# Hybrid encoder layer on one core: the input projection's x tiles 2 to 11 turned in 32x32 blocks on VectorE instead of on TensorE, the per-token scale moved to the evictions, and alternating PSUM banks

## The chip, the core and the metric

The program runs on one of the eight cores of a Trainium2 chip. A core has a matrix engine (PE, TensorE; PEld is its weight load), two engines that read and write both SBUF and PSUM (DVE, VectorE; ACT, ScalarE), a third vector engine that works in SBUF (POOL, GpSimd), a queue engine (SP) that here only issues DMAs, and 16 DMA engines. They run on their own and meet through semaphores. The metric is the device time of one execution in microseconds (us). Three executions of the kernel before took 1500.43, 1500.71 and 1501.08 us; the median is 1500.71.

## The reference, cut to what matters

One encoder layer in fp32 over a prompt of 512 tokens and a sample of 1024 tokens (1536 tokens, 12 tiles of 128), model width 1024. The change touches the part down to `proj`:

```python
h = rmsnorm(x, norm1_g)              # x * rsqrt(mean(x*x) + eps) * g
proj = h @ w_in                      # 1024 -> 1280 columns
q, k, v = proj[..., :512], proj[..., 512:640], proj[..., 640:768]
u = proj[..., 768:]                  # 512 columns for the pooling mixer
q = apply_axial_rope(rmsnorm(q, q_norm_g), cos, sin)   # per head of 64
k = apply_axial_rope(rmsnorm(k, k_norm_g), cos, sin)
a = block_swept_gqa(q, k, v)         # softmax attention, 8 q heads, 2 kv heads
p = multiscale_pool(u, w_pool, pool_scale)
x = x + concatenate([a, p]) @ w_out
x = x + square(relu(rmsnorm(x, norm2_g) @ w_up)) @ w_down
```

The token's factor rsqrt(mean(x*x) + eps) is the same for all columns of a token, so it can multiply x before the product or q, k, v and u behind it. The gain g belongs to the rows of w_in.

## The kernel before

**How the precision is kept.** Every fp32 product is made of three products of operands rounded to a shorter format: an operand is split in a rounded half (hi) and the rest (lo), and PE does hi·hi, hi·lo and lo·hi (helper `three`, lines 794 to 796). For the weights ACT writes `wihi` (the rounding, with g as its scale) and DVE `wilo` (what is left); for the tokens ACT writes `hThi` and DVE `hTlo`.

**The projection, tile by tile.** PE contracts over partitions, so each tile of x (128 tokens on partitions) has to be turned to have the 1024 model columns on partitions, as 8 blocks of 128 columns. For tile t:

- ACT squares x and sums along the row (`square_x`, L1240), POOL makes the factor `rsx` of it (`norm_x`, L2298 and L2300);
- DVE writes `xs` = x times that factor (`scale_x`, L1742);
- PE turns `xs` with 8 transposes of 128x128 into PSUM banks 0 and 1 (`transpose_x`, L803; for tile 0 L878);
- ACT rounds the result from PSUM to `hThi`, DVE takes the difference to `hTlo` (`split_hT`, L1232 and L1736);
- `project_qkv`: 48 matmuls in PSUM banks 2 and 3 give the 768 columns of q, k and v, with tokens on partitions. For each 2 tiles `project_u` gives the 512 columns of u in banks 4 and 5, with the columns on partitions and 256 tokens along the row, in four groups g of 24 matmuls.

**Behind the product.** ACT copies q and k to `qk` (`copy_qkv`), which also gives banks 2 and 3 free: the next `project_qkv` waits for `qk_copied`. ACT squares, DVE sums the squares (`sum_squares`, L1826), POOL takes the power -1/2 (`rsqk`, L2300), DVE scales (`scale_qk`, L1832) and multiplies by the gain (`gain_qk`, L1837), and then the rotation: DVE writes `roped` with the cosines (L1845), POOL writes `qsin` (L2376), DVE adds it (L1849). Then PE turns `roped` with 5 transposes (`transpose_qk`, L919) into banks 6 and 7, and ACT saves them in `QT`. u is copied from PSUM to `up` by ACT (`save_u_columns`).

**The order of the work.** It is written out by hand, engine by engine; every engine takes its instructions in order. PE's order for a pair of tiles t (even) and t+1 is: `project_qkv(t)`, `transpose_x(t+2)`, `project_qkv(t+1)`, `transpose_x(t+3)`, `project_u` of the pair with `transpose_qk(t)` ahead of its third group, `transpose_qk(t+1)`. DVE's order for a tile is V, `sum_squares(t)`, `split_hT(t+2)`, `scale_x(t+3)`, `scale_qk(t)`, `gain_qk(t)`, `rotate(t)`. The start differs: PE warms up with matmuls on zeros (L1052, twice 7), turns the column of g and tile 0, and runs tile 0 in step with the splits of the weights (`first_qkv`, L828 to L837), then tile 1 (L865 to L870); and DVE has `split_wi_u`, the rest of the weights' split (L1766), to do for the first `project_u`. In the last tiles the first attention scores are mixed into `project_u`. Behind the projection come attention (with POOL normalizing the probabilities and computing the pooling windows), the output projection and the MLP, which runs from about 600 us to the end. The change leaves them as they are.

## Time and profile before

| | |
|---|---|
| median of 3 executions | 1500.71 us (1500.43 to 1501.08) |
| span of the profiled execution, first to last instruction | 1499.2 us |
| PE busy | 1490.5 us (99% of the span) |
| DVE, ACT, POOL busy | 1015.6 (68%), 718.0 (48%), 394.7 us (26%) |
| input projection | from the start to about 200 us |

The profiled execution is one of its own; the profile gives its span and no device time beside it, and the span is 1.5 us below the median of the timed ones. In the page, "busy" is the union of an engine's instructions, and "mean ns" of a group is what one instruction took with its latency, which for pipelined matmuls is more than the distance from one start to the next. "[0.33 <-DVE xs L1742]" behind an instruction says that its engine had been idle for 0.33 us and what released it. The granted clock of PE is given as a share of full speed for each stretch; which level a matmul ran at is also seen in its own rhythm.

### The profile page before, as it was taken

What the parts mean: (1) busy time and instruction counts of PE and PEld (TensorE: products, weight loads), DVE (VectorE), ACT (ScalarE), POOL (GpSimd) and SP (SyncE); (2) the same over time, 40 slices, a digit from 0 to 9 for tenths busy, and PEclk for the clock granted to TensorE, in tenths of its full rate; (3) what the DMA queues carried; (4) which work ended last, traced back from release to release, by engine and by line L of the source; (5) the groups of instructions that cost most, each with busy time, mean ns of one, the idle gap of its engine ahead of it and who ended that gap; (6) DMA issues with size and microseconds to landing.
All of it is one profiled execution on the core that took longest, in us unless ns stands there. A gap on an engine that the chain in (4) does not pass through costs nothing.

```text
span 1499.2 us, 23419 instructions
## 1 busy us (share of the span) xinstructions
PE 1490.5 (99%) x8031; PEld 1328.7 (89%) x8031; DVE 1015.6 (68%) x1287; ACT 718.0 (48%) x1215; POOL 394.7 (26%) x348
## 2 busy tenths in 40 slices
PE   9999999999999999999999999999999999999999
PEld 8999988888878889999999999999888888888887
DVE  7434489999965567445445444548888878878875
ACT  6323289999943335555445455546332323223220
POOL 3356379988940000000000000000411311311300
PEclk9999999999999999999999999999999999999999
DMA  6110021100145737523333432438743443442434
GB/s 237 50 36 18 18 78 29 29 11 11 33 171 182 266 142 305 236 101 143 135 128 112 156 138 101 146 132 314 266 151 119 133 154 104 143 158 94 144 99 182
DMA packets 69113, 195.19 MB, mean 130 GB/s; under 512 B 5560, under 2 KB 7744, under 8 KB 68928
## 3 DMA queue, kind: packets, MB, share of 16 engines
q1 hardware_dynamic: 66992, 183.36, 34.8%
q10 hardware_dynamic: 2064, 11.08, 1.8%
q8 instruction: 35, 0.57, 0.2%
q14 instruction: 22, 0.18, 0.0%
HBM read 119.97 MB, written 67.63 MB: 125 GB/s over the span
## 4 chain that ended last, share of the span: by engine, by line
PE 93%; ACT 2%; POOL 2%; DVE 1%; issue 1%; DMA 0%; SPq 0%; ACTq 0%; POOLq 0%; DVEq 0%
PE ps L794 24%; PE ps L796 23%; PE ps L795 23%; PE ps L1096 6%; PE ps L974 4%; PE ps L1106 3%; PE ps L956 2%; PE ps L958 2%; PE ps L989 2%; PE ps L990 2%; ACT prob L1327 1%; PE ps L1116 1%; PE ps L803 1%; POOL prob L2401 0%; ACT pThi L1232 0%
## 5 line engine op out<-in xcount | busy, mean ns | idle before, releaser
L794 PE MATMUL ps<-h,wuhi 128*128 128x384 f32 (+1 forms) x904 | 301.3, 333 | 0.2 <-issue 0.2
L796 PE MATMUL ps<-h,wulo 128*128 128x384 f32 (+1 forms) x904 | 301.1, 333 | 0.0
L795 PE MATMUL ps<-h,wuhi 128*128 128x384 f32 (+1 forms) x904 | 301.1, 333 | 0.0
L794 PE MATMUL ps<-wdhi,hidhi 128*128 128x512 f32 x672 | 261.5, 389 | 0.1
L796 PE MATMUL ps<-wdhi,hidlo 128*128 128x512 f32 x672 | 261.4, 389 | 0.0
L795 PE MATMUL ps<-wdlo,hidhi 128*128 128x512 f32 x672 | 261.4, 389 | 0.0
L2202 DVE TENSOR_TENSOR yacc<-yacc,ps 128x1024 f32<-128x1024 f32 x167 | 203.3, 1217 | 77.1 <-PE ps L796 77.0
L1232 ACT ACTIVATE hidhi<-hin 128x1024 fp32r<-128x1024 f32 (+1 forms) x72 | 86.9, 1207 | 300.8 <-PE ps L796 291.7
L2116 DVE TENSOR_TENSOR u<-u,ps 128x384 f32<-128x384 f32 x96 | 53.1, 553 | 181.2 <-PE ps L796 181.1
L794 PEld LDWEIGHTS ps<-h,wuhi 128*128 128x128 f32 x904 | 169.7, 188 | 0.6 <-issue 0.4
L795 PEld LDWEIGHTS ps<-h,wuhi 128*128 128x128 f32 x904 | 169.7, 188 | 0.0
L796 PEld LDWEIGHTS ps<-h,wulo 128*128 128x128 f32 x904 | 169.7, 188 | 0.0
L794 PEld LDWEIGHTS ps<-wdhi,hidhi 128*128 128x128 f32 x672 | 126.2, 188 | 26.9 <-issue 0.5
L796 PEld LDWEIGHTS ps<-wdhi,hidlo 128*128 128x128 f32 x672 | 126.2, 188 | 26.1
L795 PEld LDWEIGHTS ps<-wdlo,hidhi 128*128 128x128 f32 x672 | 126.2, 188 | 26.0
L2573 POOL TENSOR_TENSOR hout<-h,hout 128x384 f32<-128x384 f32 x1 | 1.8, 1774 | 477.2 <-PE ps L796 477.2
L1736 DVE TENSOR_TENSOR hidlo<-hin,hidhi 128x1024 fp32r<-128x1024 f32 (+1 forms) x72 | 113.0, 1569 | 5.4 <-ACT hidhi L1232 5.4
L1736 DVE TENSOR_TENSOR pTlo<-ps,pThi 128x512 fp32r<-128x512 f32 x160 | 107.3, 687 | 13.3 <-ACT pThi L1232 11.4
L1563 ACT ACTIVATE hout<-u 128x384 f32<-128x384 f32 x96 | 50.5, 526 | 124.9 <-DVE u L2116 113.5
L1232 ACT ACTIVATE pThi<-ps 128x512 fp32r<-128x512 f32 x160 | 95.0, 600 | 18.8 <-PE ps L974 13.4
L974 PEld LDWEIGHTS ps<-ident,prob 128*128 128x128 f32 x640 | 78.3, 140 | 25.7 <-DVE pTlo L1736 3.1
L2401 POOL TENSOR_SCALAR prob<-prob,rinv 128x1024 f32<-128x1024 f32 (+1 forms) x96 | 94.4, 995 | 22.5 <-DVE rinv L1815 20.7
(221 smaller groups left out, 2822.1 us busy)
## 6 DMA issues: line engine op xcount, KB each, us to landing
hd<-hout SPq DMA_DIRECT2D x64, 384.0 KB, 3.2
hin<-hd SPq DMA_DIRECT2D x48, 512.0 KB, 3.7
hd<-hout SPq DMA_DIRECT2D x32, 576.0 KB, 2.8
hin<-hd SPq DMA_DIRECT2D x24, 768.0 KB, 4.3
wuraw<-in_w_up SPq DMA_DIRECT2D x17, 1024.0 KB, 6.0
wdraw<-in_w_down SPq DMA_DIRECT2D x8, 2048.0 KB, 9.5
h<-h2d ACTq DMA_DIRECT2D x7, 1536.0 KB, 10.9
x2in<-in_x SPq DMA_DIRECT2D x12, 512.0 KB, 3.4
```

The costliest lines, as they stand in the source:

```text
L794: pe.matmul(out, w_hi, m_hi, start=start, stop=False, skip_group_check=resumed)
L795: pe.matmul(out, w_hi, m_lo, start=False, stop=False, skip_group_check=resumed)
L796: return pe.matmul(out, w_lo, m_hi, start=False, stop=stop, skip_group_check=resumed)
L974: mm = pe.transpose(ps[:, 4 + k % 3, qt * P:(qt + 1) * P], prob[s.parity(pair, idx)][:, u, c0:c0 + P], ident[:])
L1096: pe.matmul(ps[:, 2 * i + h], c[i][:, k], wohi[:, j, h * 512:(h + 1) * 512], start=(j == 0 and c is chi), stop=False)
L1106: mm = pe.matmul(ps[:, 2 * i + h], chi[i][:, SLOT_ROWS[j]], wolo[:, j, h * 512:(h + 1) * 512], start=False, stop=(n == KT - 1))
L1232: return act.activation(out, in_, ACT.Copy, **kw)
L1563: act.activation(out, src, ACT.Relu).then_inc(relu_done, 1)
L1736: return dve.tensor_tensor(out, a, b.bitcast(F32), ALU.subtract)
L2116: dve.tensor_tensor(u, u, up_bank(par, (1, 4, 5)[k]), ALU.add).then_inc(u_sum, 1)
L2202: dve.tensor_tensor(q, q, down_banks(u, o), ALU.add).then_inc(acc_done, 1)
L2401: ins = pool.tensor_scalar(p, p, rinv[:, b, q:q + 1], 1.0, ALU.mult, ALU.mult)
```

## The change

- The model columns are dealt to partitions in another way: partition p now holds columns 8p to 8p+7, the eighth k of them in block k (before: block k holds columns 128k to 128k+127). w_in and g are loaded to fit.
- Tiles 2 to 11: SP loads x in four quarters of 256 columns to 32 partitions each (`load_x`), so that DVE can make the whole turn of 128x1024 by one STREAM_TRANSPOSE of 32x32 blocks, from SBUF to SBUF (`turn_x`). Its input is read at steps of 8 elements. `scale_x` and `transpose_x` go. `split_hT` reads `xT` in SBUF.
- Tiles 0 and 1 are turned on PE as before, but unscaled and from columns 8 elements apart (`row_in`), and without waiting for the squares.
- The squares of tiles 2 to 11 need rows of x that a second DMA brings (`load_rows`).
- The token's factor `rs` is now kept for all tiles and multiplies q, k and v when ACT and DVE take them from PSUM. For u it has to lie along the row: two DMAs for each pair of tiles write two columns of `rs` to DRAM and read them back to all partitions (`turn_rs`, `rsb`), and DVE, not ACT, takes u from PSUM, multiplied by it.
- `project_qkv` alternates between banks 0, 1 and 2, 3.
- At the start: 8 warming matmuls, not 14, and no transpose for g.

The core of the diff:

```diff
--- before.py
+++ after.py
+        rs = at("rs", X + 2048, [TT])
+        g1c = at("g1c", 1408, [KT])
+        rsb = at("rsb", X, [2, 2 * P])
+        rsd = nc.dram_tensor("rsd", [TT // 2, P, 2], F32).ap()
...
+        xT = at("xT", W + 8192, [KT, P])
...
-            k0, k1, bank = ((0, 2, 5), (2, 4, 0), (4, 8, 1))[h]
+            k0, k1, bank = ((0, 2, 6), (2, 4, 7), (4, 8, 2))[h]
...
+        def turned(t):
+            return psw[:, 2048:3072].rearrange("p (k c) -> p k c", k=KT) if t == 1 else xT[:]
+        def row_in(i, k):
+            return xin[:, i].rearrange("p (c k) -> p k c", k=KT)[:, k]
+        def quarter_in(i, q):
+            return xin[q * 32:q * 32 + 32, i].rearrange("t (b c) -> t b c", b=4)
+        def quarter_of(t, q):
+            return x[t * P:(t + 1) * P, q * 256:q * 256 + 256].rearrange("(b t) c -> t b c", b=4)
+        def blocks_in(i, k0=0, k1=KT):
+            return xin[:, i].rearrange("p (b c k) -> p k b c", b=4, k=KT)[:, k0:k1]
+        def blocks_out(k0=0, k1=KT):
+            return xT[:, k0:k1].rearrange("p k (b t) -> p k b t", b=4)
...
+        def stat_area():
+            return up[:, :, UPW - PAD - 256:UPW - PAD]
+        def qkv_banks(i):
+            return 2 * (i % 2)
+        w_rows = w_in.rearrange("(p k) n -> k p n", k=KT)
...
-                sp.wait_ge(xs_done, t - 1)
-                sp.dma_start(xin[:, i], x[bass.ds(t * P, P)]).then_inc(x_in[i], 16)
+            def load_x(t):
+                sp.wait_ge(xT_done, t - 1)
+                if t < 4:
+                    sp.wait_ge(ssx_done, t - 1)
+                for q in range(4):
+                    sp.dma_start(quarter_in(t % 2, q), quarter_of(t, q)).then_inc(x_in[t % 2], 16)
+            def load_rows(t):
+                sp.wait_ge(ssx_done, t)
+                sp.dma_start(stat_area(), x[t * P:(t + 1) * P].rearrange("t (g c) -> t g c", g=GROUPS)).then_inc(xn_in, 16)
...
+            def turn_rs(p):
+                sp.wait_ge(rsx_done, 2 * p + 2)
+                sp.dma_start(rsd[p], rs[:, 2 * p:2 * p + 2]).then_inc(rs_out, 16)
+                if p >= 2:
+                    sp.wait_ge(u_saved, FIRST + p - 1)
+                sp.wait_ge(rs_out, 16 * (p + 1))
+                if p:
+                    sp.wait_ge(rs_in, 16 * p)
+                sp.dma_start(rsb[:, p % 2], rsd[p].rearrange("t i -> (t i)").partition_broadcast(P)
+                             ).then_inc(rs_in, 16)
...
+            sp.dma_start(xin[:, 0], x[0:P]).then_inc(x_in[0], 16)
...
-            sp.wait_ge(x_in[1], 16)
...
-            load_x(2, 0)
...
+            load_wi_u(0)
+            load_wi_u(1)
             sp.dma_start(gqkb[:], gqk.partition_broadcast(P)).then_inc(gqk_in, 16)
-            sp.dma_start(rope[:, 0], rope_d[0]).then_inc(rope_in[0], 16)
-            sp.dma_start(rope[:, 1], rope_d[1]).then_inc(rope_in[1], 16)
-            load_x(3, 1)
+            load_rope(0)
+            load_x(2)
+            load_rope(1)
+            load_rows(2)
+            load_x(3)
+            turn_rs(0)
...
+            for t in range(TT):
+                if t + 4 < TT:
+                    load_x(t + 4)
+                if t + 3 < TT:
+                    load_rows(t + 3)
+                if t % 2 and t + 2 < TT:
+                    turn_rs((t + 1) // 2)
+                if t + 2 < TT:
+                    load_rope(t + 2)
...
-            def transpose_x(t):
-                pe.wait_ge(xs_done, t + 1)
-                pe.wait_ge(hT_lo, t)
-                for k in range(KT):
-                    mm = pe.transpose(psw[:, k * P:(k + 1) * P], xs[:, k * P:(k + 1) * P], ident[:])
-                mm.then_inc(xT_done, 1)
...
+            def project_qkv(t, i):
+                buf, tok, bank = i // 2, (i % 2) * P, qkv_banks(i)
+                pe.wait_ge(hT_lo, t + 1)
+                pe.wait_ge(qk_copied, FIRST + t - 1)
...
+                for k in range(KT):
+                    if k == 5:
+                        pe.wait_ge(x_in[1], 16)
+                        for c in range(KT):
+                            mm = pe.transpose(turned(1)[:, c], row_in(1, c), ident[:])
+                        mm.then_inc(xT_done, 1)
+                    if k in (0, 2):
+                        pe.wait_ge(hT_hi_half, 1 + k // 2)
                     if k == 4:
                         pe.wait_ge(hT_hi, 1)
+                    high(k)
+                    if k in (0, 2):
+                        pe.wait_ge(hT_lo_half, 1 + k // 2)
+                    if k == 4:
                         pe.wait_ge(hT_lo, 1)
-                    high(k)
                     cross(k)
-                    if k == 5:
-                        transpose_x(1)
-                    mm = low(k)
-                mm.then_inc(qkv_done, 1)
+                    if k:
+                        low(k - 1)
+                low(KT - 1).then_inc(qkv_done, 1)
...
-                transpose_x(2)
-                def between(g):
-                    if g == 2:
-                        pe.wait_ge(v_lo, FIRST + 2)
-                        transpose_x(3)
-                    if g == 3:
-                        transpose_qk(0, 0)
-                pe.wait_ge(qk_copied, FIRST + 2)
-                project_u(0, 0, between)
+                project_u(0, 0, lambda g: transpose_qk(0, 0) if g == 3 else None)
...
-                transpose_x(4)
                 project_qkv(3, 3)
-                transpose_x(5)
...
-                    project_qkv(t, i, 0 if last and i == 2 else 2)
-                    if not (last and i >= 2):
-                        transpose_x(t + 2)
+                    project_qkv(t, i)
...
-            warm(7)
...
+            split_first(0)
+            act.wait_ge(g1_in, 16)
             split_wi(0)
-            split_first(0)
+            split_first(1)
             split_wi(1)
-            split_first(1)
+            split_first(2)
             split_wi(2)
-            split_first(2)
             split_wi(3)
             split_wi(4)
-            square_x(1, 1)
-            for k in range(5, KT):
-                split_wi(k)
+            square_x(0)
+            split_wi(5)
             split_hT(1, 1)
-            square_x(2, 0)
+            split_wi(6)
+            split_wi(7)
+            square_x(1)
...
+                copy(qk[:].rearrange("p h d -> p (h d)"), psw[:, bank * 512:bank * 512 + QKW],
+                     scale=rs[:, t:t + 1]).then_inc(qk_copied, 1)
+                copy(V[:, t, :, 0:HEAD], ps[:, bank + 1, P:2 * P].rearrange("p (v d) -> p v d", v=NKV),
+                     scale=rs[:, t:t + 1]).then_inc(v_hi, 1)
...
-            def save_u_columns(n, i):
-                p = n * 2 + i // 2
-                act.wait_ge(u_done, FIRST + p + 1)
-                act.wait_ge(pads, 1)
-                if isinstance(n, int) and p == TT // 2 - 1:
-                    act.wait_ge(ssx_done, TT)
-                copy(up[:, :, bass.ds(p * 256 + PAD + 2 * PAD * ((n + 1) // 2), 256)],
-                     psw[:, 2048:3072].rearrange("p (g c) -> p g c", g=GROUPS)).then_inc(u_saved, 1)
...
-            def scale_x(t, i):
-                dve.wait_ge(rsx_done, t + 1)
-                dve.wait_ge(xT_done, t)
-                dve.tensor_scalar(xs[:], xin[:, i], rsx[:, 0:1], 1.0, ALU.mult, ALU.mult).then_inc(xs_done, 1)
+            def turn_x(t):
+                dve.wait_ge(x_in[t % 2], 64 * (t // 2) + 16)
+                dve.wait_ge(hT_hi, t)
+                dve.wait_ge(hT_lo, t)
+                dve.transpose(blocks_out(), blocks_in(t % 2)).then_inc(xT_done, 1)
...
+            def save_u_columns(p):
+                dve.wait_ge(u_done, FIRST + p + 1)
+                dve.wait_ge(rs_in, 16 * p + 16)
+                dve.wait_ge(pads, 1)
+                if p == TT // 2 - 1:
+                    dve.wait_ge(ssx_done, TT)
+                c0 = p * 256 + PAD + 2 * PAD * (p >= SEQ_P // 256)
+                dve.tensor_tensor(up[:, :, c0:c0 + 256].rearrange("p g (i t) -> p g i t", i=2),
+                                  psw[:, 2048:3072].rearrange("p (g i t) -> p g i t", g=GROUPS, i=2),
+                                  rsb[:, p % 2].rearrange("p (t i) -> p i t", i=2).unsqueeze(1).to_broadcast([P, GROUPS, 2, P]),
+                                  ALU.mult).then_inc(u_saved, 1)
...
-                scale_x(2, 0)
                 for k in range(KT // 2):
                     split_wi_u(k)
                 scale_qk(0)
                 for k in range(KT // 2, KT):
                     split_wi_u(k)
-                split_v(1, 5)
                 dve.wait_ge(gq_scaled, 1)
                 gain_qk(0)
+                split_v(1, 3)
                 sum_squares(1)
+                rotate(0, 0)
+                turn_x(2)
                 split_hT(2, 2)
-                scale_x(3, 1)
-                rotate(0, 0)
                 scale_qk(1)
                 gain_qk(1)
+                turn_x(3)
+                rotate(1, 1)
                 split_hT(3, 3)
-                rotate(1, 1)
-                scale_x(4, 0)
+                turn_x(4)
+                save_u_columns(0)
...
-                        scale_x(t + 3, (i + 3) % 2)
+                    if t + 3 < TT:
+                        turn_x(t + 3)
...
+                    if i % 2 and not (last and i == 3):
+                        save_u_columns(t // 2)
...
+            save_u_columns(TT // 2 - 1)
...
-                    if not (last and i >= 1) and not opens:
-                        norm_x(t + 3)
...
+                    if t + 2 < TT:
+                        norm_x(t + 2)
```

DVE, the first pair of tiles behind the split of the weights, before (`qn<-qk,rsqk` is scale_qk(1), the last two rows are rotate(1) but for its neighbours; the number behind a name is its buffer):

```order
L1736 TENSOR_TENSOR V<-ps,V 128x2x64
L1837 TENSOR_TENSOR qn<-qn,gqkb 128x640
L1826 TENSOR_REDUCE ssqk<-qksq 128x10
L1736 TENSOR_TENSOR hTlo_83<-ps,hThi_81 128x8x128
L1742 TENSOR_SCALAR xs<-xin,rsx 128x1024
L1845 TENSOR_TENSOR roped<-qn,rope 128x640
L1849 TENSOR_TENSOR roped<-roped,qsin 128x640
L1832 TENSOR_TENSOR qn<-qk,rsqk 128x640
L1837 TENSOR_TENSOR qn<-qn,gqkb 128x640
L1736 TENSOR_TENSOR hTlo_83<-ps,hThi_81 128x8x128
L1845 TENSOR_TENSOR roped<-qn,rope 128x640
L1849 TENSOR_TENSOR roped<-roped,qsin 128x640
```

The same place now:

```order
L1842 TENSOR_TENSOR qn<-qn,gqkb 128x640
L1824 SCALAR_TENSOR_TENSOR V<-ps,rs,V 128x2x64
L1831 TENSOR_REDUCE ssqk<-qksq 128x10
L1850 TENSOR_TENSOR roped<-qn,rope 128x640
L1854 TENSOR_TENSOR roped<-roped,qsin 128x640
L1756 STREAM_TRANSPOSE xT<-xin 128x1024
L1749 TENSOR_TENSOR hTlo_84<-xT,hThi_82 128x8x128
L1837 TENSOR_TENSOR qn<-qk,rsqk 128x640
L1842 TENSOR_TENSOR qn<-qn,gqkb 128x640
L1756 STREAM_TRANSPOSE xT<-xin 128x1024
L1850 TENSOR_TENSOR roped<-qn,rope 128x640
L1854 TENSOR_TENSOR roped<-roped,qsin 128x640
```

`rotate(0)` stands ahead of the work on tile 2, and two STREAM_TRANSPOSE stand where two TENSOR_SCALAR stood and one place on; `gain_qk(0)` has changed places with V.

PE, from the last matmuls of `project_qkv(2)` into `project_qkv(3)`, before:

```order
L795 MATMUL ps<-wilo,hThi_81 128x256
L796 MATMUL ps<-wihi,hTlo_83 128x256
L803 MATMUL ps<-ident,xs 128x128 x8
L794 MATMUL ps<-wihi,hThi_81 128x512
L795 MATMUL ps<-wilo,hThi_81 128x512
L796 MATMUL ps<-wihi,hTlo_83 128x512
```

And now:

```order
L850 MATMUL ps<-wilo,hThi_82 128x256
L851 MATMUL ps<-wihi,hTlo_84 128x256
L849 MATMUL ps<-wihi,hThi_82 128x512
L850 MATMUL ps<-wilo,hThi_82 128x512
L851 MATMUL ps<-wihi,hTlo_84 128x512
```

The eight transposes between the two products are gone; the products' own matmuls stand as they did.

## Rows read from the trace of the kernel before

**Rows 1.** The page's busy times by engine.
```profile
PE 1490.5 (99%) x8031; PEld 1328.7 (89%) x8031; DVE 1015.6 (68%) x1287; ACT 718.0 (48%) x1215; POOL 394.7 (26%) x348
```

**Rows 2.** Stretches: us, then busy us (and instructions) of each engine, clock, DMA, GB/s.
```profile
10.00:20.00 10.00, 9.77 (x56) 7.89 (x55) 8.79 (x11) 9.04 (x14) 1.59 (x4) 1.00 1.04 400
...
100.00:120.00 20.00, 19.85 (x122) 17.51 (x121) 5.77 (x7) 5.07 (x8) 14.97 (x19) 1.00 0.10 30
120.00:140.00 20.00, 19.87 (x154) 19.05 (x153) 10.09 (x12) 5.78 (x9) 13.93 (x16) 1.00 0.09 34
```

**Rows 3.** Groups of instructions on PE from 0 to 215 us: busy, mean ns.
```profile
L803 PE MATMUL ps<-ident,xs 128*128 128x128 f32 x88 | 11.5, 273 | 0.0
```

**Rows 4.** Timeline of PE around a turn between two qkv products.
```profile
50.46 1.04 PE L803 MATMUL ps<-ident,xs 128*128 128x128 f32 x8
51.51 0.47 PE L794 MATMUL ps<-wihi,hThi 128*128 128x512 f32 x1
51.81 0.40 PE L795 MATMUL ps<-wilo,hThi 128*128 128x512 f32 x1
```
**Rows 5.** Timeline of ACT: a rounding of tile 2, and a copy that frees banks.
```profile
29.11 1.03 ACT L1232 ACTIVATE hThi<-ps 128x1024 fp32r<-128x1024 f32 x1
...
50.66 0.70 ACT L1232 ACTIVATE qk<-ps 128x640 f32<-128x640 f32 x1 [7.34 <-PE ps L796]
```
**Rows 6.** Timeline of PE around a turn between a qkv product and u.
```profile
91.25 1.03 PE L803 MATMUL ps<-ident,xs 128*128 128x128 f32 x8
92.04 0.36 PE L794 MATMUL ps<-hThi,wihi 128*128 128x256 f32 x1
```

**Rows 7.** The chain that ended last, from 95 to 105 us: start, us, what.
```profile
95.25 0.54 POOL rsx L2300
96.06 2.48 POOL rsqk L2300
...
102.80 1.61 DVE roped L1849
104.46 0.77 PE ps L919 x5
```

**Rows 8.** Groups on DVE from 0 to 215 us, by form.
```profile
L1736 DVE TENSOR_TENSOR hTlo<-ps,hThi 128x1024 fp32r<-128x1024 f32 x11 | 13.4, 1219 | 0.4
...
L1742 DVE TENSOR_SCALAR xs<-xin,rsx 128x1024 f32<-128x1024 f32 x11 | 8.2, 749 | 3.5 <-POOL rsx L2300 3.5
```

**Rows 9.** Timeline of DVE, the first pair of tiles.
```profile
26.59 0.83 DVE L1832 TENSOR_TENSOR qn<-qk,rsqk 128x640 f32<-128x640 f32 x1 [1.20 <-POOL rsqk L2300]
...
40.62 0.83 DVE L1849 TENSOR_TENSOR roped<-roped,qsin 128x640 f32<-128x640 f32 x1 [1.68 <-POOL qsin L2376]
```
**Rows 10.** Timeline of PE at the same place.
```profile
41.50 0.77 PE L919 MATMUL ps<-ident,roped 128*128 128x128 f32 x5
```

**Rows 11.** Timeline of POOL at the start.
```profile
22.68 0.85 POOL L2326 TENSOR_SCALAR gqkb<-gqkb 128x512 f32<-128x512 f32 x1 [2.89 <-DMA gqkb<-in_gqk]
```

**Rows 12.** Timeline of ACT at the start.
```profile
7.05 0.94 ACT L1232 ACTIVATE wihi<-wraw,g1c 128x768 fp32r<-128x768 f32 x1 [1.68 <-DMA wraw<-in_w_in]
```
**Rows 13.** Timeline of PE at the start.
```profile
4.96 2.40 PE L1052 MATMUL ps<-zeros 128*128 128x512 f32 x7
7.20 1.03 PE L878 MATMUL ps<-ident,xs 128*128 128x128 f32 x8
8.31 0.62 PE L828 MATMUL ps<-wihi,hThi 128*128 128x512 f32 x2
```
**Rows 14.** The warming matmuls of PE: ns min/median/max, first and last start.
```profile
L1052 PE MATMUL ps<-zeros x14: 389/628/796, 1.5 to 7.0; 128*128 128x512 f32 x14
```

**Rows 15.** Timeline of PE at the end of the projection.
```profile
202.36 0.63 PE L974 MATMUL ps<-ident,prob 128*128 128x128 f32 x4 [0.28 <-issue]
```
**Rows 16.** Timeline of POOL there.
```profile
198.00 4.16 POOL L2401 TENSOR_SCALAR prob<-prob,rinv 128x512 f32<-128x512 f32 x6 [0.82 <-DVE rinv L1815]
...
206.34 1.37 POOL L2401 TENSOR_SCALAR prob<-prob,rinv 128x512 f32<-128x512 f32 x2 [0.94 <-DVE rinv L1815]
```

193 lines of the change are left out of this document (69 added, 124 removed).

## The prediction

> **What bounds the kernel now.** I read the busy times first [rows 1]: PE is busy for 1490.5 of 1499.2 us, so nearly every microsecond that PE works less, or waits less, is one of the kernel, and what the others do counts only where PE comes to wait for it. Then the stretches of the projection [rows 2]: PE stands for 0.15 and 0.13 us in 20, DVE works 6 to 10 of 20 us and ACT 5 to 6, so both have room; POOL is fuller (14 to 15). The granted clock is 1.00 in each of these stretches. Then PE's groups [rows 3]: the turns of x are 88 matmuls (and 8 more for tile 0) with 11.5 us of busy time, 0.131 us each; the 273 ns beside it is latency, not cost. Last the chain [rows 7], since it shows what is nearly late: rsx and rsqk on POOL, and then the rotation's addition on DVE (102.80, 1.61 us) released PE's transposes at 104.46. The addition ends at 104.41, just when PE comes. So at each odd tile the rotation is level with PE, and a PE that comes earlier can run into it. That is the question here.
>
> **What PE no longer does.** Tiles 4 to 11, eight of them, cost two different amounts. Between two qkv products (tiles 4, 6, 8, 10) the eight transposes start at 50.46 and the next product at 51.51: 1.05 us [rows 4]. Part of that is not transposing but the copy that frees the banks: ACT's copy runs from 50.66 to 51.36 [rows 5]; with alternating banks this wait goes as well, since the product then needs the copy of the tile before last. Ahead of u (tiles 5, 7, 9, 11) it is 92.04 - 91.25 = 0.79 us [rows 6]. Behind the transposes the first product matmul takes 0.47 against 0.40 us [rows 4], so I add 0.07 each time. 4 x (1.05 + 0.79 + 2 x 0.07) = 7.9 us. By the group's mean it would be 8 x 1.05 = 8.4, by the starts alone 7.4; those are its ends. The warming matmuls and g's transpose fall in PE's wait for the first weights and are worth nothing by themselves.
>
> **Tiles 2 and 3: PE's gain turns into a wait.** They would save another 1.7 us (2 x 0.86). But `transpose_qk(1)` starts at 41.50 [rows 10] and the addition it needs ends at 40.62 + 0.83 = 41.45 [rows 9]. PE cannot pass there before rotate(1) is done, so I work out DVE's row. In the old order from `scale_qk(0)` (26.59) to the end of that addition are 14.9 us. Out of it go split_hT(3) (1.22, which now follows rotate(1)), scale_x(3) (0.75) and the waits of 1.68 and about 0.3 us, less some 0.15 of overlap: 3.8. In come two turns of T each, a wait for ACT's rounding of tile 2, which can only begin when the turn is done (1.03 [rows 5], 1.1 with the two hand-overs), about 1.2 of waiting for POOL's qsin of tile 0 (it starts behind norm_x(2), which comes now between rsqk and qsin) and 0.7 for that of tile 1. With T = 1.2 that is 5.4, so 1.6 us longer. Against it, scale_qk(0) starts earlier: POOL's row of rsqk(0) stands behind the scaling of gqkb, which waited for its DMA until 22.68 [rows 11], and tile 2's 512 KB no longer go ahead of it in the queue (1.3 us at the 400 GB/s of [rows 2]). Sum +0.3; with 0.3 for what I can't see of POOL and DVE holding each other up, rotate(1) ends at about 42.0 and PE passes **0.6 us later** than before, having stood for some 2.7 us. Ends: -0.3 (turns as short as scale_x, 0.75) to +2.6 (turns of 2.2).
>
> **The turn itself, T.** The trace has no STREAM_TRANSPOSE. Near rows of the same 128x1024 on DVE are 0.749 us (one input, scale_x) and 1.219 us (two inputs, one from PSUM) [rows 8]. I take the slower, T = 1.2, since nothing here shows that a turn can go at the pace of a plain scaling. For the range 0.75 to 2.4: the faster row below, and above twice the slower one, because the input steps by 32 bytes, which no row does.
>
> The Trainium skill speaks against the change at this point: "SBUF — State Buffer", section "Door 1: The DMA port swizzle", says that SBUF is read at full rate only while at least two accesses fall in a 16-byte line, that is, up to steps of four fp32; steps of eight would pay on every element. No run shows by how much; the rival below prices a turn of twice the row.
>
> **Steady tiles: is the rotation still in time?** Before, from the end of an odd qkv product to PE's need are 104.46 - 92.04 = 12.4 us, 12.1 without the stall; it stays so. Now POOL takes rsqk first and norm_x after it, which takes about 1.9 us out of the even tile's chain (it used to wait for ACT's square); the rotation of an even tile then ends about 10.2 us behind its product, 1.8 behind the next one's end. The odd tile's own chain from there is V, sum (1.1), rsqk at +1.3, and from rsqk's start to the end of the addition 104.41 - 96.06 = 8.35 [rows 7]: 1.8 + 1.3 + 8.35 = 11.4 us against 12.1. It holds, with 0.7 us in hand, as DVE's hT and turn (1.15 + 1.2 behind the sum) end before rsqk does (2.5). So the stalls of [rows 2], 0.28 us together, go. `save_u_columns` is 1.2 us more on DVE for a pair, behind rotate, where DVE waits for the next product: hidden. The x quarters, rows and two small DMAs of each pair (14 issues for two tiles against 4, the rope tables among them) are asked for a tile or more ahead; SP has nothing else to do.
>
> **The start.** The first weights land at 7.05 [rows 12] whatever PE does, and from there ACT and DVE set the pace of tile 0 (each k needs a split of 0.94 us on ACT and one on DVE). Tile 0 is turned before 7 us instead of at 7.20 to 8.23 [rows 13]; first_qkv then ends 0.4 us sooner at best, which the wait at rotate(1) swallows. A PE that is late by 1 us or so here is swallowed too. 0.
>
> **The end of the projection.** ACT no longer copies u before QT, so the first transposes of attention lose their 0.28 us [rows 15]. DVE takes u at u_done, ahead of two reciprocals, so POOL's last two normalizations slip by about 2.7 us behind 202.1 [rows 16]; POOL has waits from 206.34 on (0.94 and more [rows 16]) to make up for it before PE asks. -0.28.
>
> **Sum** against the profiled execution: -7.9 - 0.28 - 0.28 + 0.6 = -7.9; 1499.2 - 7.9 = 1491.3 us of span. The timed median lies 1.5 us above that span, so 1500.7 - 7.9 = **1492.8 us**.
>
> **Rivals.**
> *Slow turns (2.0 to 2.4 us).* For it: the 32-byte step. At T = 2.2 the passage at rotate(1) is 2.0 later. In the steady tiles DVE's scale then waits for the turn and not for rsqk: the even tile ends 0.9 later, the odd one's turn ends 0.7 behind its rsqk, 11.4 + 1.6 = 13.0 against 12.1. That is 0.9 of stall at tiles 5 and 7; at 3 and 9, where the addition is not stretched from 0.83 to 1.61 by POOL's window sums, 0.1 to 0.2. Together 4.1: 1496.9.
> *PE at 1.2 GHz at the start.* The 14 warming matmuls ran mostly at the lower level (median 628 ns [rows 14]) and changed only in the second seven, which took 2.40 us from 4.96 [rows 13], while the first had taken up to 3.4 (1.5 to 4.96); now there are 8, then transposes, then a wait of about 1 us for weights. If the products begin at the lower level they take twice as long until it rises. For some 3 us that is 1.5 to 3 us late at tile 0, of which the wait at rotate(1) takes 1: +1.3, so 1494.1. The Trainium skill, "TensorE: Matmul & The Clock Gate", section "Part 4: PE-mode transpose", says that the full clock doesn't engage for transposes. That is this rival; nothing in this trace decides it.
> *Slower than before: DVE becomes the bound.* One mechanism: a turn of 4 us. Then DVE's turns set each pair's length: the odd rotation ends 13.0 + 2 x 1.8 = 16.6 us behind its product, against 12.1: 4.5 of stall at tiles 5 and 7, 3.7 at 3, 2.7 at 9 (its even tile alone has a turn), and 2 x 2.8 = 5.6 at rotate(1). 21 - 7.9 = +13: 1514. It outweighs the gain from T of about 2.6 us. Against it: no DVE row of this size takes over 1.22 us.
> *The change doesn't bring what it says*, because another wait of 5 us or more takes the place of the transposes (rsb's two DMAs in series behind SP's other waits, or quarters landing late): the stage is as long as before, 1500. Against it: the factor of a pair is ready a whole product before u is, and x comes two tiles ahead.
>
> **Chances.** Forecast 0.68, slow turns 0.13, low clock 0.09, DVE-bound 0.06, nothing gained 0.04. A measurement tells 0.2%, 3 us, from no change: faster means below 1497.7. Faster: 0.68 + 0.09 + 0.09 of the slow turns = 0.86; same 0.08; slower 0.06. The forecast's own range is 1490.8 to 1494.5 (7.4 or 8.4 for the transposes, and -0.3 to +2.6 at rotate(1)); to leave out no more than 2 in 10 it goes up to the slow turns: 1490.5 to 1497.
>
> **What would show it.** The transposes of x on PE are 16, not 96; PE busy falls by about 10 us, of which some 2 come back as idle time before the transposes of roped(1), released by DVE roped (stall 2 to 3 us at about 39 to 42 us). The second qkv product of a pair starts right at the end of the first. STREAM_TRANSPOSE has a mean near 1.2 us; 2 or more would be the slow rival. PE idle in 100 to 140 us is below 0.1. The warming matmuls and first products show by their length (0.40 or 0.8 for 512 columns) whether the clock was up. If PE stands at roped of tiles 5 and 7, the estimate of the steady margin is wrong; if idle time is put down to DMA or to `up`, the last rival holds.

## The result, and the profile after

| kernel | median us (lowest to highest) | ratio to before | profiled span | time around the span | PE busy | clock |
|---|---|---|---|---|---|---|
| before | 1500.71 (1500.43 to 1501.09) | 1 | 1499.2 | about 1.8 | 1490.5 | 1.000 |
| changed | 1507.24 (1506.39 to 1507.53) | 1.0041 (1.0028 to 1.0054) | 1505.3 | 2.2 | 1482.3 | 0.997 |

The kernel became slower by 6.5 us; 1492.8 was forecast, with a range that ended at 1497.0. The page's busy line of the changed kernel answers to [rows 1]:

```profile
PE 1482.3 (98%) x7944; PEld 1320.4 (88%) x7944; DVE 1037.8 (69%) x1289; ACT 713.9 (47%) x1207; POOL 400.9 (27%) x347
```

PE is busy 8.2 us less, where the forecast had about 10 (7.9 for tiles 4 to 11, the rest for tiles 2 and 3); the difference is about what the lower clock, read below, adds to the busy time. And PE is idle 23.0 us instead of 8.7. The windows say where (columns: stretch, length, then busy time of PE, PEld, DVE, ACT and POOL with their counts, granted clock, DMA share, GB/s); the middle ones stand beside [rows 2]:

```profile
20.00:40.00 20.00, 19.57 (x144) 18.32 (x142) 15.86 (x20) 9.28 (x15) 9.97 (x9) 1.00 0.56 106
40.00:60.00 20.00, 12.06 (x57) 10.48 (x58) 8.13 (x7) 4.01 (x6) 2.40 (x4) 0.74 0.46 123
100.00:120.00 20.00, 19.06 (x136) 17.75 (x135) 9.52 (x10) 2.96 (x5) 16.56 (x19) 1.00 0.36 93
140.00:160.00 20.00, 19.22 (x118) 17.29 (x119) 8.77 (x9) 6.09 (x11) 15.54 (x19) 1.00 0.17 37
160.00:180.00 20.00, 19.22 (x140) 18.04 (x139) 10.06 (x13) 5.76 (x9) 7.39 (x7) 1.00 0.21 40
600.00:620.00 20.00, 18.53 (x108) 18.24 (x107) 5.99 (x11) 7.86 (x17) 0.00 (x0) 1.00 0.82 325
```

Some 8 us are gone between 40 and 60, with a mean clock of 0.74; 0.8 to 0.9 in each stretch with an odd tile; 1.5 in a place that the change doesn't touch. PE's row shows the transposes of q and k of tiles 1, 5, 7 and 9 (start, duration, operation, in brackets the idle time before it and who ended it), which answer to [rows 7, 10]:

```profile
47.94 1.33 PE L955 MATMUL ps<-ident,roped 128*128 128x128 f32 x5 [8.32 <-DVE roped L1854]
110.32 0.77 PE L955 MATMUL ps<-ident,roped 128*128 128x128 f32 x5 [0.94 <-DVE roped L1854]
140.78 0.76 PE L955 MATMUL ps<-ident,roped 128*128 128x128 f32 x5 [0.95 <-DVE roped L1854]
171.07 0.76 PE L955 MATMUL ps<-ident,roped 128*128 128x128 f32 x5 [0.78 <-DVE roped L1854]
```

The first is followed back in four queues. SP, ACT, POOL and DVE, in this order:

```profile
36.46 2.51 SPq L574 DMA_DIRECT2D xin<-in_x  x4
39.02 0.55 SPq L579 DMA_DIRECT2D up<-in_x  x1
...
43.26 1.06 ACT L1275 ACTIVATE up<-up 128x1024 f32<-128x1024 f32 x1 [5.73 <-DMA up<-in_x]
...
44.48 0.19 POOL L2319 TENSOR_TENSOR msx<-ssx,epsx 128x1 f32<-128x1 f32 x1 [8.27 <-ACT up L1275]
44.75 0.55 POOL L2321 TENSOR_TENSOR rs<-msx,mexp 128x1 f32<-128x1 f32 x1
45.27 0.87 POOL L2392 TENSOR_TENSOR qsin<-qn,rope 128x320 f32<-128x320 f32 x1
...
34.31 2.12 DVE L1756 STREAM_TRANSPOSE xT<-xin 128x1024 f32<-128x1024 f32 x1
40.29 2.00 DVE L1756 STREAM_TRANSPOSE xT<-xin 128x1024 f32<-128x1024 f32 x1
42.22 0.78 DVE L1850 TENSOR_TENSOR roped<-qn,rope 128x640 f32<-128x640 f32 x1
47.06 0.82 DVE L1854 TENSOR_TENSOR roped<-roped,qsin 128x640 f32<-128x640 f32 x1 [4.06 <-POOL qsin L2392]
```

SP stands at the quarters of tile 4, which wait for the turn of tile 2 (34.31 + 2.12 = 36.43). Behind them in its queue stand the rows of tile 3. They are asked for at 39.02 and land at 43.2; ACT squares them, POOL's norm of tile 3 waits for that, and the sine products of tile 1, which need nothing of tile 3, stand behind the norm. Their operands had been there since 40.4. The rotation of tile 1 ends at 47.9, where PE was ready at 39.6.

Then PE runs slower. Windows around the wait:

```profile
42.00:44.00 2.00, 0.00 (x0) 0.00 (x0) 1.00 (x2) 0.74 (x1) 0.00 (x0) 0.65 0.45 138
44.00:46.00 2.00, 0.00 (x0) 0.00 (x0) 0.00 (x0) 1.94 (x4) 1.44 (x3) 0.50 0.87 208
48.00:52.00 4.00, 4.00 (x12) 3.38 (x13) 3.87 (x3) 0.70 (x1) 0.00 (x0) 0.50 0.07 21
52.00:54.00 2.00, 2.00 (x8) 1.60 (x7) 0.33 (x1) 0.00 (x0) 0.00 (x0) 0.79 0.43 109
```

The granted clock is at 0.50, its lower level of 1.2 GHz, until about 52.7, some 5 us after PE has work again. From the transposes of tile 1 to those of tile 2 it takes 25.34 us (47.94 to 73.28); from tile 3 to tile 4, the same work, 23.03 (79.89 to 102.92). So the clock costs 2.3 us.

The group of the turn, which no row of before could show (to be held against [rows 8]):

```profile
L1756 DVE STREAM_TRANSPOSE xT<-xin 128x1024 f32<-128x1024 f32 x10 | 21.3, 2129 | 1.1
```

2.13 us a turn, where 1.2 was taken; the rival "slow turns" had 2.2.

Landmarks of PE, after minus before: transposes of tile 0 -2.0, of tile 1 +6.4, tile 3 +7.0, tile 5 +5.9, tile 7 +4.7, tile 9 +3.6, tile 11 +3.7, end +6.1. The gain of the removed transposes is visible: from the transposes of an odd tile to those of the next even one it takes 2.0 us less than before, and 0.8 of that go to the wait at the next odd one. On balance 3.7 us are lost in the projection and 2.4 behind it (0.4 up to the start of the MLP, 1.5 in the one wait at 617 us).

### The profile page after: what moved, and what is told of

Same layout as the page of the kernel before. It is cut to its first block, busy times and chain, and to the rows that moved or that the text cites. A ratio compares the mean times of both kernels' runs of the same rounds, so it can differ in the third digit from the quotient of the medians.

```text
span 1505.3 us, 23234 instructions
## 1 busy us (share of the span) xinstructions
PE 1482.3 (98%) x7944; PEld 1320.4 (88%) x7944; DVE 1037.8 (69%) x1289; ACT 713.9 (47%) x1207; POOL 400.9 (27%) x347
## 4 chain that ended last, share of the span: by engine, by line
PE 58%; DMA 1%; DVE 1%; issue 0%; ACT 0%; ACTq 0%; DVEq 0%
PE ps L849 19%; PE ps L850 19%; PE ps L851 19%; DMA hd<-hout 1%; DVE wulo L1749 0%; DVE yacc L2223 0%; DVE hout L2149 0%; ACT hout L1576 0%; ACT hidhi L1263 0%; DVE wdlo L1749 0%; ACT hout L1578 0%; DVE hidlo L1749 0%; DVE wuraw L2091 0%; DVE yacc L2230 0%; ACT u L1263 0%
## 5 line engine op out<-in xcount | busy, mean ns | idle before, releaser
L1263 ACT ACTIVATE pThi<-ps 128x512 fp32r<-128x512 f32 x160 | 94.9, 600 | 18.9 <-PE ps L1008 13.4
```

The costliest lines, as they stand in the source:

```text
L1263: return act.activation(out, in_, ACT.Copy, **kw)
```

## Experiments

Medians in us. The kernel before, run beside them, took 1501.2 beside e1, e2, e3 and b1, 1501.1 beside e4 to e7, 1501.2 beside e8, e9, e10 and b2, and 1500.9 beside b3 and e11; each ratio is to those. "Wait at tile 1" is PE's idle time before that tile's transposes, "rest" what lies between those of tile 11 and the end of the profiled span, "wait at 610" the longest wait of PE on ACT's copy u in the up stage. The last three columns are of the one profiled execution, which can lie off the median: by +1.7 us in e10, +3.1 in e11, -0.6 in e9.

| run | edit | us | ratio (95%) | wait at tile 1 | rest | wait at 610 |
|---|---|---|---|---|---|---|
| before | | 1500.71 | | 0 | 1298.8 | 0 |
| changed | | 1507.24 | 1.0028 to 1.0054 | 8.32 | 1301.2 | 1.5 |
| e1 | rows of tile 3 asked for early | 1502.64 | 1.0001 to 1.0020 | 4.50 | 1301.7 | 1.6 |
| e2 | norm of tile 3 behind the sines | 1506.26 | 1.0022 to 1.0044 | 6.41 | 1303.2 | 2.1 |
| e3 | PE kept busy in the wait | 1504.65 | 1.0012 to 1.0030 | 2.16 | 1299.4 | 0.6 |
| b1 | before, 1 of 8 transposes left | 1501.58 | 0.9994 to 1.0012 | 0 | 1299.5 | 0.6 |
| e4 | turn with unit step | 1506.93 | one run | 8.41 | 1303.6 | 2.4 |
| e5 | DVE's order in odd steps | 1507.71 | 1.0032 to 1.0059 | 8.95 | 1302.9 | 2.0 |
| e6 | e1, turn 3 late, ACT saves early | 1502.18 | 1.0000 to 1.0018 | 3.93 | 1301.6 | 1.5 |
| e7 | all queues reordered but PE's | 1499.80 | 0.9984 to 1.0002 | 2.55 | 1301.0 | 1.5 |
| e8 | PE's order only | 1493.29 | 0.9938 to 0.9965 | 0.64 | 1300.6 | 0.9 |
| e9 | e8, e1, ACT saves early | 1491.98 | 0.9931 to 0.9959 | 0 | 1300.1 | 0.9 |
| e10 | e9, new DRAM buffer last | 1492.34 | 0.9927 to 0.9954 | 0 | 1302.8 | 2.0 |
| b2 | before, DRAM buffer added | 1501.04 | 0.9991 to 1.0010 | 0 | 1298.8 | 0 |
| b3 | before, x in quarters | 1501.37 | 0.9993 to 1.0011 | 0 | 1298.9 | 0 |
| e11 | e9 with one pair of banks | 1498.20 | 0.9972 to 0.9991 | 0 | 1304.0 | 2.3 |

**e1, the rows of tile 3 early.**

```
             sp.dma_start(pscale[:], pool_scale).then_inc(pool_in, 16)
+            load_rows(3)
             for t in range(TT):
                 if t + 4 < TT:
                     load_x(t + 4)
-                if t + 3 < TT:
+                if t and t + 3 < TT:
                     load_rows(t + 3)
```

> The changed kernel with one edit on SP: the statistics rows of tile 3 are asked for before the x quarters of tile 4, not behind them. Theory A (the rotation of tile 1 waits on the rows' transfer: SP stands at the quarters of tile 4 until the turn of tile 2 has ended at 36.4 us, the rows land at 43.2, ACT squares them, POOL's norm of tile 3 follows at 44.5 and its sine products of tile 1, queued behind it, only at 45.3): the rows land before 37 us, the sine products start when the gain has ended, about 40.4, DVE's add at 43.0, PE's transposes of tile 1 at about 43.8 with 4.2 us of idle time in place of 8.3; 1507.2 - 4.1 = 1503.1 us, and down to 1500.7 if the 2.4 us that the lower granted clock cost from 43 to 53 us go too. Theory B (the two turns of 2.13 us in front of the rotation hold it, and the transfer lies beside them): no change, 1507 us, PE still at about 48.

Measured 1502.64. PE stands at the transposes of tile 1 at 43.47, theory A's 43.8, and theory B is out. But the trace names another releaser, and ACT's row shows why:

```profile
43.47 1.30 PE L956 MATMUL ps<-ident,roped 128*128 128x128 f32 x5 [4.50 <-ACT QT L1264]
...
41.68 1.06 ACT L1264 ACTIVATE hThi<-xT 128x1024 fp32r<-128x1024 f32 x1 [3.79 <-DVE xT L1757]
42.64 0.69 ACT L1264 ACTIVATE QT<-ps 128x640 f32<-128x640 f32 x1
```

ACT's save of tile 0 frees the bank into which tile 1 is transposed, and stands in the queue behind the split of tile 3, which waits for DVE's second turn. With the transfer gone, the slow turn is the next thing on the path, on two queues at once. That order of ACT was in no term of the forecast.

**e2, the norm of tile 3 behind the sine products of tile 1** (POOL alone; two lines moved).

> The changed kernel with one edit on POOL: the norm of tile 3 stands behind the sine products of tile 1 instead of in front of them; SP's queue is left as it is, so the rows of tile 3 still land at about 43. Theory A: only the order on POOL carries the wait to the rotation, so it is cut here as well: sine products at 40.4, PE at about 43.8, 1500.7 to 1503.1 us as when the rows are asked for early. Theory B: 1507 us. A variant of A in which ACT's queue matters too (the split of tile 3 stands behind the square that waits for the rows until 44.4): the product of tile 3 would start late; by the trace the low half of tile 3 would be ready at about 46.6 and PE needs it at about 53, so no idle time there.

Measured 1506.26, where 1500.7 to 1503.1 was expected: a miss. PE starts at 45.58 instead of 43.8. POOL's link is cut (the sine products ran at 39.99), but the same late transfer reaches PE over ACT:

```profile
42.75 1.06 ACT L1275 ACTIVATE up<-up 128x1024 f32<-128x1024 f32 x1 [5.70 <-DMA up<-in_x]
...
43.81 1.04 ACT L1263 ACTIVATE hThi<-xT 128x1024 fp32r<-128x1024 f32 x1
44.75 0.68 ACT L1263 ACTIVATE QT<-ps 128x640 f32<-128x640 f32 x1
```

The expectation looked at ACT's queue, but only for the split of tile 3 and not for the save behind it. One late transfer held two queues: with one of them cut PE starts 2.4 us sooner than in the changed kernel, with the cut at the source 4.5 us.

**e3, PE kept busy in the wait.**

```
+                pe.wait_ge(v_lo, FIRST + 1)
+                for _ in range(30):
+                    pe.matmul(ps[:, 0], hThi[0][:, 0, 0:P], wihi[:, 0, 0:512], start=True, stop=True)
                 transpose_qk(1, 1)
```

> The changed kernel with 30 extra products (128x128 by 128x512, into a bank that the next product overwrites, about 0.23 us each, 7 us) on PE in front of the transposes of tile 1: they fill the 8.3 us in which PE waits, and nothing else is moved. Theory C (the idle time itself makes the granted clock fall to 0.50 from 43 to 53 us, and that costs 2.4 us beyond the wait): clock 1.00 from 36 to 60 us, the transposes of tile 1 still at 47.9, the stretch from there to the transposes of tile 2 23.0 us in place of 25.3; 1507.2 - 2.4 = 1504.8 us. Theory D (the products of this stretch are slow for another reason, such as the two turns and transfers beside them): the clock may stay up, but the stretch still takes 25.3 us, 1507 us.

Measured 1504.65, the expected number, but by other terms, so by luck. The products filled 7.0 us and 2.16 were left idle. The clock still fell, later, as the length of the products behind it shows (0.63 us each in place of 0.39):

```profile
47.69 0.77 PE L958 MATMUL ps<-ident,roped 128*128 128x128 f32 x5 [2.16 <-DVE roped L1857]
48.53 0.45 PE L850 MATMUL ps<-wilo,hThi 128*128 128x512 f32 x1
49.20 0.63 PE L849 MATMUL ps<-wihi,hThi 128*128 128x512 f32 x1
51.33 0.63 PE L851 MATMUL ps<-wihi,hTlo 128*128 128x512 f32 x1
52.17 0.39 PE L850 MATMUL ps<-wilo,hThi 128*128 128x512 f32 x1
```

The stretch to tile 2 takes 24.66 us, 0.7 less than in the changed kernel and 1.6 more than at full clock. Of the 2.8 us between the two profiled spans that is 0.7; 0.3 lie in front of the transposes of tile 1, and 1.8 behind the projection (0.9 of them a shorter wait at 610), where the edit does nothing. So neither theory as it stands: the length of the products says that the lost 2.3 us are the lower clock, as C has it, but a wait of 2.2 us was followed by the lower clock too, and the expected 1.00 was not seen. The price was 1.6 us here. It doesn't go by the length of the wait, as e4 shows.

**b1, the kernel before with one transpose of eight** for tiles 4 to 11.

> The kernel before with 7 of the 8 PE transposes of each of tiles 4 to 11 left out (the evictions then read old values of PSUM; everything else stands). It prices what the change takes off PE, without anything that it adds. Theory E (the transposes were on PE's path in full, 1.05 and 0.79 us for 8): 7/8 of 7.9 us less, minus stalls that appear at the odd tiles, where the rotation ended level with PE at 104.4 us: each odd tile 5, 7, 9 loses up to 0.9 us of the 0.9 that it gained before its rotation. Sum -6.9 us with no stalls, -4.2 with them: 1493.8 to 1496.5 us. Theory F (the rotation chain of each pair is the real bound and the transposes lay beside it): no change, 1500.7 us.

Measured 1501.58, no gain at all, where E expected 4.2 to 6.9 us. E had the waits at the rotation right and missed a second kind:

```profile
PE ps L794 <- ACT qk L1232: 3.1, 4, 0.8
PE ps L919 <- DVE roped L1849: 2.1, 3, 0.9
```

(Columns: engine, tile and line, who is waited for, then us in total, times, longest.) Of the 6.9 us that E prices, 3.1 return before the odd products, which come to the PSUM banks before ACT has evicted the even tile, and 2.1 before the odd rotations, and the wait at 610 takes 0.6 more; the last 1.1 us are not accounted for. At tile 11 PE is 0.7 us ahead of the kernel before. So there the transposes were cover. That they are worth something only with alternating banks is what e11 tests.

**e4, a turn that reads with unit step.**

```
-            return xin[:, i].rearrange("p (b c k) -> p k b c", b=4, k=KT)[:, k0:k1]
+            return xin[:, i].rearrange("p (k b c) -> p k b c", b=4, k=KT)[:, k0:k1]
```

> The changed kernel, with DVE's transpose reading the quarters of x with a step of 4 bytes between the elements of a block row instead of 32 (the rows of x then reach the product in another order than the weights', which is left wrong here). Theory G (the 32-byte step makes the turn slow): the turn of 128x1024 falls from 2.13 us to the 1.07 to 1.2 us that DVE's copies and subtractions of this size take. Theory H (the transpose has a price of its own per element, whatever the step): it stays at 2.0 to 2.2 us. On the time of the kernel: the idle time of 8.3 us at tile 1 stays under both (it waits for the rows' transfer); under G the waits at tiles 5, 7 and 9 lose only some 0.1 to 0.2 us each, since POOL's reciprocal root ends 0.13 us before the turn does; 1506.5 to 1507 us against 1507.2.

```profile
L1756 DVE STREAM_TRANSPOSE xT<-xin 128x1024 f32<-128x1024 f32 x10 | 12.4, 1244 | 1.1
```

Theory G: 2.13 us became 1.24, the step alone makes the turn 0.9 us longer. The time, 1506.93 in a single execution, lies within the spread of the changed kernel and says nothing by itself; the waits at tiles 5, 7 and 9 fell to 0.58, 0.60 and 0.47, by 0.3 to 0.4 us each and not by the 0.1 to 0.2 expected, and that at tile 3 (0.16) went. The Trainium skill, "SBUF — State Buffer", section "Door 1: The DMA port swizzle", says that accesses which don't share a 16-byte line with another lose the full rate; the trace agrees, by a factor of 1.71 at a step of 32 bytes.

This run also shows what the price of the clock does not hang on. PE waits 8.41 us at tile 1, as long as in the changed kernel, and the clock goes to 0.50 in the wait, but it is back 2.7 us after PE has work again, not after about 5:

```profile
50.00:52.00 2.00, 2.00 (x9) 1.62 (x9) 0.95 (x1) 0.00 (x0) 0.00 (x0) 0.96 0.13 23
```

The stretch to tile 2 takes 24.33 us (47.39 to 71.72), 1.3 more than at full clock, against 2.3 in the changed kernel. Over the runs with more than 2 us of wait at tile 1 the price is 1.3 to 2.3 us, and it doesn't rise with the wait (2.16 us: 1.6; 4.50: 1.3; 8.41: 1.3; 8.32: 2.3).

**e5, DVE's order at tiles 3, 5 and 7.**

> The changed kernel with another order on DVE at tiles 3, 5 and 7: the low half of tile t+2 is taken behind the gain of tile t (beside POOL's sine products) and the turn of tile t+3 behind the rotation of tile t, in place of both in front of the scale. Nothing of tile 1 is touched. Theory I (in the odd steps what DVE does between the sum and the scale delays the rotation, by the turn's last 0.1 us and by POOL's first addition, which takes 1.12 us beside the subtraction of the low half and 0.21 us elsewhere): the scale starts 0.9 us sooner, the waits of PE at tiles 5 and 7 (0.94 and 0.95 us) go, tile 9 keeps 0.78; 1507.2 - 2.0 = 1505.2 us. Theory J (POOL's reciprocal root, the sine products and the addition set the chain, whatever stands between): waits as before, 1507.2 us. If the low half slows POOL's sine products instead, half of the gain is lost.

Measured 1507.71 where theory I expected 1505.2; the waits at tiles 5 and 7 went from 0.94 and 0.95 to 0.85 and 0.87, and the 0.16 at tile 3 went. The last sentence of the expectation named the reason and priced it too low: not half of the gain was lost but nearly all. The rows of tile 5 show both sides. POOL's first addition beside DVE's subtraction of the low half, in the kernel before, in the changed kernel, and in this run, where the subtraction has moved away:

```profile
94.84 1.21 DVE L1736 TENSOR_TENSOR hTlo<-ps,hThi 128x1024 fp32r<-128x1024 f32 x1
95.76 0.21 POOL L2298 TENSOR_TENSOR msqk<-ssqk,epsqk 128x10 f32<-128x10 f32 x1
...
101.04 1.22 DVE L1749 TENSOR_TENSOR hTlo<-xT,hThi 128x1024 fp32r<-128x1024 f32 x1
101.20 1.12 POOL L2319 TENSOR_TENSOR msqk<-ssqk,epsqk 128x10 f32<-128x10 f32 x1 [2.00 <-DVE ssqk L1831]
...
100.67 0.21 POOL L2323 TENSOR_TENSOR msqk<-ssqk,epsqk 128x10 f32<-128x10 f32 x1 [2.00 <-DVE ssqk L1831]
104.71 3.21 POOL L2396 TENSOR_TENSOR qsin<-qn,rope 128x320 f32<-128x320 f32 x2 [0.54 <-DVE qn L1842]
```

The subtraction of the kernel before read `ps` in PSUM, and POOL's addition ran beside it in 0.21 us. The changed one reads `xT` in SBUF, and the addition takes 1.12 us. That 0.9 us in front of the reciprocal root is a cost of the change that is not the turn. Here it is gone, and the sine products take 3.21 us instead of 2.35 (see e7).

**e6, the turn of tile 3 behind the rotation, ACT's save first.**

> The kernel with the rows of tile 3 asked for early (1502.6 us, PE idle 4.5 us at tile 1, then released by ACT's copy of the transposed q and k of tile 0, which stood behind the split of tile 3 and so behind DVE's turn of tile 3), with two edits more: ACT makes that copy before the square and the split of tile 3, and DVE turns tile 3 behind the rotation of tile 1. Theory A continued (with the transfer out of the way it is the slow turn in front of the rotation, on DVE and through ACT's queue): the addition of tile 1 ends at 42.3 instead of 43.1, PE is idle 3.3 us in place of 4.5, and of the 1.4 us that the lower clock still costs some goes: 1502.6 - 1.2 = 1501.4 us, down to 1500.5. Rival K (DVE's turn of tile 3 is then late for the product of tile 3): PE would wait before that product; by the trace it needs the low half at about 52 and gets it at 46, so no wait.

Measured 1502.18, PE at 42.75 with 3.93 us idle, where 3.3 was expected. That is 0.5 of the 1.2 us expected, and 0.5 us between these two runs is not clear of noise. No wait before the product of tile 3, so K is out.

**e7, every queue but PE's.**

> The changed kernel with every wait of PE in front of tile 1 and in the odd steps worked on: rows of tile 3 asked for early; ACT saves tile 0 before it squares tile 3; POOL scales the gain vector after the reciprocal root of tile 0 and takes the norm of tile 3 behind the sine products of tile 1; DVE scales and gains tile 1 before it takes the low half of tile 2, and turns tile 3 behind the rotation; at tiles 3, 5 and 7 the order of the steady-order experiment. Theory A with the terms of the traces: the rotation of tile 1 ends at about 39 to 40, when PE comes, so 8.3 us of idle time and the 2.4 us of lower clock go (-10.7), and up to 2.0 us in the odd steps: 1494.5 us, at least 1497 if a wait of 2 us is left at tile 1. That would be below the kernel before (1500.7 us): the gain that was forecast was there and was lost to the order of the queues. Rival L (a fifth of the loss or more is elsewhere, in the stretch after the projection, where the trace of the changed kernel shows 2.4 us more than before, 1.5 of them at one wait on ACT at 617 us): that part stays, 1496 to 1499 us.

Measured 1499.80, 5.3 us above the 1494.5. A wait of 2.55 us is left at tile 1 and the clock falls again (1.6 us), the waits at tiles 5, 7 and 9 are still 0.84, 0.83 and 0.77, and the part behind the projection is as long as in the changed kernel, as L has it. POOL's row against DVE's shows what was overlooked:

```profile
37.22 3.19 POOL L2397 TENSOR_TENSOR qsin<-qn,rope 128x320 f32<-128x320 f32 x2 [1.84 <-DVE qn L1843]
...
37.06 1.22 DVE L1750 TENSOR_TENSOR hTlo<-xT,hThi 128x1024 fp32r<-128x1024 f32 x1
38.20 1.50 DVE L1851 TENSOR_TENSOR roped<-qn,rope 128x640 f32<-128x640 f32 x1
```

The same pair of sine products took 1.69 us beside a turn (39.79 in e1) and beside nothing on DVE (45.27 in the changed kernel), and 3.19 beside these two; the cosine product lost as well, 1.50 us instead of 0.82. The Trainium skill, "SBUF — State Buffer", section "SBUF: two separate sides", says that POOL and DVE have one pair of ports in common, and that whichever starts first, a DVE operation with two SBUF inputs or a POOL operation that reads SBUF, holds it alone until it ends. The trace agrees: the subtraction and the cosine product have two such inputs, the turn one. So the low half can't hide beside POOL's products, and the turn can.

**e8, PE's order alone.** The transposes of an odd tile stand behind the next tile's product.

```
-                transpose_qk(1, 1)
                 project_qkv(2, 2)
+                transpose_qk(1, 1)
...
                     project_qkv(t, i)
+                    if not i % 2:
+                        transpose_qk(t - 1, 1)
...
-                        transpose_qk(t, i)
+                        if t == TT - 1:
+                            transpose_qk(t, i)
```

> The changed kernel with one edit on PE: the transposes of q and k of every odd tile t stand behind the q, k, v product of tile t+1 instead of in front of it; queues, DVE, POOL and ACT as in the changed kernel. Theory N (all that was lost in the projection is PE standing in front of the rotation of the odd tiles, first because of the rows' transfer, then because of the chain of sum, root, scale, sine products and addition; the work of the product covers it): PE starts the product of tile 2 at about 39.2, when its low half is ready (38.8), and comes to the transposes of tile 1 at 47.6 to 48, when the addition has ended (47.9); no idle time over 1 us at tile 1, none at tiles 5, 7, 9, no lower clock: 1507.2 - 8.3 - 2.4 - 2.7 = 1493.8 us; up to 1496 where the product of tile 3 now waits for its low half, which DVE takes behind that addition (ready at 49.0, wanted at 48.4) and ACT's late copies shift the even tiles. Theory O (the waits only move: what is not ready for the transposes is not ready for the following product either): PE idle about as long, 1503 to 1507 us.

Measured 1493.29 (1493.8 expected). Theory N. The transfer is as late as in the changed kernel and the turn as slow, but PE has 8.4 us of product to do meanwhile; 0.64 and 0.37 us of waiting are left, none at tiles 3 to 9, and the clock stays at 1.00:

```profile
48.02 0.76 PE L954 MATMUL ps<-ident,roped 128*128 128x128 f32 x5 [0.64 <-DVE roped L1856]
49.15 0.50 PE L849 MATMUL ps<-wihi,hThi 128*128 128x512 f32 x1 [0.37 <-DVE hTlo L1751]
```

**e9, with the rows early as well.**

> The same order on PE, with the rows of tile 3 asked for before the quarters of tile 4 and ACT saving tile 0 before it squares tile 3. Theory N: the low half of tile 3 is then ready at about 45, so the last wait of the first block goes too: 0.5 to 2 us below the run with PE's order alone, 1492 to 1494 us. Theory O: no better than that run.

Measured 1491.98, a ratio of 0.9945 (0.9931 to 0.9959): below both kernels. The 1.3 us to e8 are of the size expected (tile 11's transposes come 1.5 us sooner), though the two intervals overlap. In the projection PE has no gap left from 40 us on:

```profile
40.00:60.00 20.00, 20.00 (x130) 18.24 (x130) 15.78 (x16) 8.60 (x13) 7.95 (x9) 1.00 0.44 119
100.00:120.00 20.00, 20.00 (x135) 18.50 (x134) 9.69 (x12) 7.92 (x13) 14.27 (x17) 1.00 0.32 75
```

**e10, b2 and b3, on the part behind the projection.**

> The same kernel as e9, with its one new DRAM buffer (rsd, 6 KB, the token scales on their way) allocated behind the buffers of the hidden layer instead of in front of them, so that these lie where they lay in the kernel before. Theory P (the 1.5 to 2.4 us that PE waits on ACT at about 600 to 617 us in nearly all versions of the changed kernel, and the 2.4 us that the part behind the projection is longer in all, come from the shifted addresses of the stores and loads there): that wait falls to 0 to 0.6 us and the time is 1.5 to 2.5 us below e9. Theory Q (it is a race of the stores with the weights' loads that falls out by the moment, and the address has nothing to do with it): same time as e9 within 0.7 us.

> The kernel before with a DRAM buffer of the same 6 KB added in front of its others and never used; no instruction differs. Theory P: it gains the wait of 1.5 to 2.4 us at about 612 us: 1502.5 to 1503.5 us. Theory Q, or a buffer that is not laid out because nothing uses it: 1501.0 us as before.

> The kernel before with each of the x transfers of tiles 2 to 11 cut into four quarters of the columns (packets of 1 KB, as in the changed kernel, to the same place); nothing else is changed. It asks where the rest of the changed kernel's loss comes from, the 2.4 us behind the projection, of which PE spends 1.5 waiting on ACT at 617 us, behind a store that landed late. Theory R (the more and smaller transfers on SP's queue in the projection leave the queue or the engines in a state in which the stores of the up stage land later): the wait on ACT at about 612 us grows from 0 to 1 to 2 us, 1502.5 us. Theory Q (that wait falls out by the moment, and the transfers of the projection have no part in it): 1501.1 us as before, since the x of a tile is asked for a whole tile ahead there.

Measured 1492.34, 1501.04 and 1501.37. e10 still has a wait of 2.0 us at 603 us, so P is out, and b2 and b3 have none there, so neither the new DRAM buffer nor the cutting of the x transfers into quarters brings it by itself (b3 has lost its 0.5 us by the transposes of tile 1, 42.02 against 41.50). Whether the unused buffer of b2 was laid out is not known; e10 doesn't hang on that. The other new transfers, the rows of x and the two small DMAs of each pair, were not tried.

**e11, one pair of banks for tiles 2 to 8.**

> The kernel e9 (odd transposes behind the next product, rows asked for early; 1492.0 us) with the q, k, v products of tiles 2 to 8 all in the PSUM banks 0 and 1, as the kernel before had them in one pair, with the waits that this needs; tiles 9 to 11 alternate. Theory S (without x transposes between the products PE comes to the odd product before ACT has evicted the even one, as in the kernel before with one transpose of eight, where four products waited 0.8 us each for the copy of q and k; only the alternation makes the removed transposes worth their time): the products of tiles 3, 5 and 7 wait 0.8 us each, and up to 1.8 us where ACT first saves the transposed tile in front of that copy: 1492.0 + 2.4 to 5.4 = 1494.4 to 1497.4 us. Theory T (the alternation is a detail, the copy is hidden by the transposes of q and k that now stand there): 1492 us.

Measured 1498.20, 6.2 us above e9 and 0.8 above the range of theory S. T is out:

```profile
PE ps L850 <- ACT qk L1266: 4.7, 3, 1.6
PE ps L850 <- ACT u L1266: 2.6, 2, 2.3
```

Three products wait 1.6 us each, 4.7 in all, and PE comes to the transposes of tile 11 6.0 us later than in e9. The profiled execution lies 3.1 us above the median, and the rest of its loss (3.9 us behind the projection, 1.4 of them in the wait at 610) is not to be put down to the banks. The alternation is no detail of the change.

## Why the prediction was wrong

*PE is the bound, and the removed transposes were on its path: right.* The stretch of a pair in which they stood became 2.0 us shorter, the 7.9 / 4 of the forecast. The forecast counted ACT's copy only as a part of the 1.05 us between two products; b1 shows that the transposes covered an eviction of some 0.8 us more for each pair, and e11 that the alternating banks stand in for that cover.

*Tiles 2 and 3, a wait of 2.7 us at the rotation of tile 1: this is the step that failed.* It rested on "the x quarters, rows and two small DMAs of each pair are asked for a tile or more ahead; SP has nothing else to do". SP has little to do and yet stands: at the first pair the rows of tile 3 are behind transfers that wait for DVE's turn of tile 2. I counted the DMAs and not the queue. What stands behind a waiting instruction was counted for PE and POOL, and left out for SP and for ACT's save of tile 0. PE was ready at 39.6, as the forecast had it (42.1 less 2.7), but the rotation ended at 47.9 and not at 42.0: PE waited 8.3 us instead of 2.7 (+5.6). e1 moved the rows alone, and PE came 4.5 us sooner; what was then left over the forecast was the slow turn.

*The clock.* The forecast weighed the lower level at the start only; there the rival "PE at 1.2 GHz" did not come. The windows give 1.00 at the start even for the warming matmuls, which took 645 ns each, so the products' own length decides, and the first two took 0.59 us, against 0.62 in [rows 13]:

```profile
6.82 0.59 PE L874 MATMUL ps<-wihi,hThi 128*128 128x512 f32 x2 [0.72 <-ACT wihi L1263]
```

The lower level came behind the wait instead, where it cost 2.3 us that stand in no term. The rule of the Trainium skill, "TensorE: Matmul & The Clock Gate", section "Part 4: PE-mode transpose", that the full clock doesn't engage for transposes, made no product late at the start, although eight transposes stood right in front of them.

*T = 1.2 us: mis-sized, 2.13.* That is the rival "slow turns" (2.2 at 1496.9). It called 0.9 us at tiles 5 and 7 (measured 0.94, 0.95) and 0.1 to 0.2 at tiles 3 and 9 (measured 0.16 and 0.78). Together 2.8 us of waits at tiles 3 to 9 in place of none. With T = 1.24 (e4) 0.5 to 0.6 were left at tiles 5, 7 and 9, so T explains less than half, and the match at 5 and 7 is partly luck. The forecast's "11.4 against 12.1" is 12.5 against 12.0 in e4, from the start of ACT's copy behind the odd product (95.48) to the end of the addition (108.02). The main part of that is the "rsqk at +1.3": it came at +2.3, since POOL's first addition took 1.12 us and not 0.21 beside a subtraction that now has both inputs in SBUF (e5). That term was put at nothing. At the first pair the slow turn was in the shadow of the transfer; with that gone it held PE 4.5 us (e1).

*Start and end of the projection.* 0 and -0.3 were said. The transposes of tile 0's q and k came 2.0 us earlier, and that went into the wait at tile 1. At the end the offset stays at +3.6 to +3.7 from tile 9 to 11: nothing gained.

*Behind the projection: -0.3 was forecast, 2.4 us were lost.* All profiled versions of the changed kernel have a rest of 1299.4 to 1304.0 us, and those of the kernel before 1298.8 to 1299.5, with 0.6 to 2.4 us against 0 to 0.6 in the wait at 610, where ACT waits for stores of the hidden layer to land. Two causes were tried and did not bring it; the cause stays open. As each number is of one execution, their size is rough.

Sum: 5.6 + 2.3 + 2.8 + 2.7 (2.4, and the 0.3 that was to come) = 13.4 of the 14.0 us between the forecast span of 1491.3 and 1505.3. The rival on the slower side (DVE as the bound, T = 4) was not it, though it alone had the sign right: a turn took 2.13 us and DVE was busy for 9.5 of the 20 us from 100 on. The case "another wait takes the place" named the queue of SP, for `rsb` and the quarters and not for the rows, was given 0.04, and was priced at no more than what the transposes had brought. That was the error of judgement: a wait in a start-up stage isn't bounded by what is gained there.

## What to carry to other kernels

Where a change makes a transfer feed something on the path, read the issuing queue in order and ask for each entry what it waits for; an idle queue engine can still be the one that is late. Before repairing four queues, look whether the waiting engine has other work that is ready: moving five transposes behind the next product (e8) brought 14 us, reordering SP, ACT, POOL and DVE (e7) 7. Work that is taken off the bound engine may have covered an eviction, so price the removal by itself. And where an operand moves from PSUM to SBUF, look at what POOL does beside the operation that reads it.

## What the hardware showed that was not expected

A 32x32-block transpose of 128x1024 fp32 on DVE takes 2.13 us with a step of 32 bytes and 1.24 with unit step. A gap of 2.2 us on PE (e3) was followed by a granted clock of 0.50 too, at a price of 1.6 us; gaps of 8.3 and 8.4 us cost 2.3 and 1.3. Two POOL products of 128x320 took 1.69 us beside DVE's turn and 3.19 beside two DVE operations with two inputs in SBUF each. An addition of 128x10 on POOL took 0.21 us beside a DVE subtraction from PSUM and 1.12 beside the same subtraction from SBUF.
